# First layer's queries normalised chunk by chunk inside the projection, and turned ahead of the gating products

## The reference, cut to what matters

```
proj = h @ w_in[layer]                       # 2048 x 5632
u, v_sgu, za, q, k, v, zb = split(proj)      # 1024,1024,1024,1024,256,256,1024 columns
q = rope(rms_norm(heads(q, 8), q_norm_w))    # context rows: no rope
k = rope(rms_norm(heads(k, 2), k_norm_w))
attn = softmax(q k^T / sqrt(128)) v
s = w_sgu @ rms_norm(gelu(v_sgu), v_norm_w) + b_sgu
y = concat([gelu(u) * s * silu(za), attn * silu(zb)]) @ w_out[layer]
```

## Time and profile before

| | us |
|---|---|
| median of 3 runs (4398.26 to 4411.34) | 4401.06 |
| profiled execution, its time | 4397.11 |
| profiled execution, its span | 4395.3 |
| PE busy | 4023.3 (92%) |
| PE weight loads busy | 3134.3 (71%) |
| DVE busy | 2200.5 (50%) |
| ACT busy | 1661.2 (38%) |
| POOL busy | 139.8 (3%) |

### The profile page before, as it was taken

The page is one execution under the profiler, slowest core; times in us unless marked ns, Lnnn a source line. Parts: engine busy times, 40 slices in busy tenths (PEclk is TensorE's granted clock), DMA queues, the critical chain, the costliest instruction groups (busy, mean ns, idle before and its releaser), DMA issues. The chain is left out here.

```text
span 4395.3 us, 50269 instructions
## 1 busy us (share of the span) xinstructions
PE 4023.3 (92%) x20175; PEld 3134.3 (71%) x20175; DVE 2200.5 (50%) x3220; ACT 1661.2 (38%) x2270; POOL 139.8 (3%) x246
## 2 busy tenths in 40 slices
PE   5699999789799799977889999999995899999998
PEld 2466657668688688634677788888885777888887
DVE  6611123463544764375555555455547455554554
ACT  4221112341343444322224454354443445544543
POOL 2000000000000000002110000000000000000000
PEclk8799999899999999997769999999997999999999
DMA  9566555203265166532325565665561555656664
GB/s 355 184 214 206 196 183 172 92 24 120 72 192 166 64 213 196 158 115 90 117 84 169 145 186 191 187 185 188 189 219 59 183 175 144 186 190 189 186 198 162
DMA packets 351933, 719.05 MB, mean 164 GB/s; under 512 B 24478, under 2 KB 26874, under 8 KB 346858
## 3 DMA queue, kind: packets, MB, share of 16 engines
q1 hardware_dynamic: 331872, 637.74, 46.3%
q0 software_dynamic: 18192, 76.35, 5.1%
q10 hardware_dynamic: 1672, 2.24, 0.1%
HBM read 686.33 MB, written 26.48 MB: 162 GB/s over the span
## 5 line engine op out<-in xcount | busy, mean ns | idle before, releaser
L2187 DVE TENSOR_TENSOR ring_r<-ring,ring_r 128x1024 fp32r<-128x1024 f32 (+1 forms) x984 | 1189.6, 1218 | 1677.7 <-ACT ring_r L1496 1653.9
L1496 ACT ACTIVATE ring_r<-ring 128x1024 fp32r<-128x1024 f32 (+1 forms) x984 | 1029.6, 1053 | 1796.3 <-DMA ring<-in_w_in 587.2
L862 PE MATMUL acc<-ring_r,feat_hi 128*128 128x512 f32 x5120 | 1598.9, 394 | 32.3 <-DVE modc L2569 14.7
L862 PEld LDWEIGHTS acc<-ring_r,feat_hi 128*128 128x128 f32 x5120 | 956.5, 189 | 282.9 <-issue 32.1
L862 PE MATMUL acc<-ring_r,feat_lo 128*128 128x512 f32 x2560 | 1000.3, 391 | 0.0
L862 PE MATMUL acc<-ring_r,hid_t_hi 128*128 128x512 f32 x2048 | 631.5, 390 | 0.0
L862 PEld LDWEIGHTS acc<-ring_r,feat_lo 128*128 128x128 f32 x2560 | 482.7, 189 | 102.6
L862 PEld LDWEIGHTS acc<-ring_r,hid_t_hi 128*128 128x128 f32 x2048 | 383.7, 188 | 79.3
L862 PE MATMUL acc<-ring_r,hid_t_lo 128*128 128x512 f32 x1024 | 398.5, 389 | 0.0
L862 PE MATMUL acc<-ring_r,feat_e_hi 128*128 128x512 f32 (+1 forms) x1088 | 332.2, 388 | 17.1 <-DVEq L2275 9.8
L862 PEld LDWEIGHTS acc<-ring_r,feat_e_hi 128*128 128x128 f32 x1088 | 204.7, 191 | 58.3 <-issue 12.0
(11 more groups left out here) (453 smaller groups left out, 3268.4 us busy)
## 6 DMA issues: line engine op xcount, KB each, us to landing
ring<-in_ffn_up SPq DMA_DIRECT2D x256, 512.0 KB, 3.7
ring<-in_ffn_down SPq DMA_DIRECT2D x256, 512.0 KB, 3.9
ring<-in_w_mod SPq DMA_DIRECT2D x192, 512.0 KB, 5.4
ring<-in_w_in SPq DMA_DIRECT2D x176, 512.0 KB, 3.8
ring<-in_w_out SPq DMA_DIRECT2D x64, 512.0 KB, 3.7
ring<-in_even_w_in SPq DMA_DIRECT2D x64, 512.0 KB, 3.6
ring<-in_xattn_wkv SPq DMA_DIRECT2D x32, 512.0 KB, 5.4
ring<-in_even_w_out SPq DMA_DIRECT2D x32, 512.0 KB, 3.6
```

Source lines behind the costliest of these rows:

```text
L862: mm = pe.matmul(bank[0:l.shape[-1], 0:width], l, r, start=(kk == 0 and j == 0), stop=(kk == g.kt - 1 and j == len(terms) - 1))
L1496: f(ring_r[:, slot, 0, 0:kt, 0:width], ring[:, slot, 1, 0:kt, 0:width], ACT.Copy) \
L2187: tt(lo, raw, hi, ALU.subtract).then_inc(sem("w_lo"), E.up("w_lo"))
```

## The change

- **ACT, chunks 6 and 7 of layer 0**: a chunk's four tiles go into four buffers (two of `prob`, two of `stage`). After the fourth, ACT forms the chunk's 16 square sums into a scratch `q_tmp` (in the place of `kvb`, free until the key chunk) and their roots, and reports four tiles through `za_ready`. The first copy of chunk 6 waits for the means of v (`ms_ready`), the first of chunk 7 for the four query writes.
- **DVE**: the means of v move from the hook of chunk 5 to the front of slot 1 of chunk 6 (layer 0 only). At slots 1 to 4 of the next chunk (7 for chunk 6's heads, the key chunk for chunk 7's) it normalises and, for tiles 0 and 1, rotates one tile's four heads, then lets POOL write them.
- **POOL**: the eight writes now send normalised rows. `stage_free` comes after the last of them; w_sgu also waits for the writes. `q_d` is read back as soon as PE has used slot 3 (counted from 0) of the last `zb` chunk, when the first half of the features is free.
- **After the projection, both layers**: PE turns w_sgu, then all keys, then all queries, and then multiplies the gate; DVE copies in that order and does the gate's steps after the copies. `qk_ready` comes once, at the end of `norm_early`.

```diff
@@ POOL
-                                dma(q_d[...], prob[:, t % 2], f"q_out{t % 2}")
+                                dma(q_d[...], (prob, stage)[t // 2][:, t % 2], f"q_out{t % 2}")
...
+                if l == 0:
+                    for j in range(2):
+                        pool.wait_ge(sem(f"q_out{j}"), 16 * 4)
                 dma(sgu_raw, I["w_sgu"][l].rearrange("g p q -> p g q"), "sgu_in")
...
-                    pool.wait_ge(sem("proj_done"), L.due("proj_done"))
-                    for j in range(2):
-                        pool.wait_ge(sem(f"q_out{j}"), 16 * 4)
+                    pool.wait_ge(sem("ring_free"), slots_done(gemms["b1_0"][-2], 1, KT // 2 // KS))
                     dma(qbs[0], q_d.rearrange("(t p) d -> p t d", p=P), "q_in")
@@ PE, after the projection
+                pe.wait_ge(sem("qk_ready"), E.due("qk_ready"))
+                for t in range(4):
+                    turn([kvb[:, t, j * HD:(j + 1) * HD] for j in range(2)])
+                if l == 0:
+                    pe.wait_ge(sem("q_in"), 16)
+                for t in range(tiles):
+                    for h in (0, 4):
+                        turn([qb[:, t, (h + j) * HD:(h + j + 1) * HD] for j in range(4)])
                 pe.wait_ge(sem("sgu_t_ready"), E.due("sgu_t_ready"))
...
-                for t in range(4):
-                    pe.wait_ge(sem("qk_ready"), E.due("qk_ready"))
-                    if t < tiles:
-                        for h in (0, 4):
-                            turn([qb[:, t, (h + j) * HD:(h + j + 1) * HD] for j in range(4)])
-                    turn([kvb[:, t, j * HD:(j + 1) * HD] for j in range(2)])
@@ ACT, chunks 6 and 7 of layer 0
-                        if n_q[0] >= 2:
-                            act.wait_ge(sem(f"q_out{n_q[0] % 2}"), E.due(f"q_out{n_q[0] % 2}", 16))
-                        f(prob[:, n_q[0] % 2], bank, ACT.Copy).then_inc(sem("act_free"), E.up("act_free"))
+                        q = (prob, stage)[t // 2][:, t % 2]
+                        if n_q[0] == 0:
+                            act.wait_ge(sem("za_used"), E.due("za_used", 2))
+                            act.wait_ge(sem("ms_ready"), E.seen["ms_ready"] + 1)
+                        if n_q[0] == 4:
+                            for j in range(2):
+                                act.wait_ge(sem(f"q_out{j}"), E.due(f"q_out{j}", 32))
+                        f(q, bank, ACT.Copy).then_inc(sem("act_free"), E.up("act_free"))
+                        n_q[0] += 1
+                        if t < 3:
+                            return
...
+                        for u in range(4):
+                            act.wait_ge(sem("act_step"), E.cnt["act_step"])
+                            for h in range(4):
+                                hs, at = slice(h * HD, (h + 1) * HD), 32 + 8 * u + heads.start + h
+                                f(q_tmp[:, 0, hs], (prob, stage)[u // 2][:, u % 2, hs], ACT.Square, accum_out=stat[:, at:at + 1]) \
+                                    .then_inc(sem("act_step"), E.up())
+                        act.wait_ge(E.last_sem(), E.last_count())
+                        f(by_tile(stat2), by_tile(stat), ACT.Sqrt, bias=eps[:, 0:1], scale=1.0 / HD).then_inc(sem("act_step"), E.up())
+                        act.wait_ge(E.last_sem(), E.last_count())
+                        for u in range(4):
+                            act.nop().then_inc(sem("za_ready"), E.count("za_ready"))
@@ ACT, after the projection
-                if l == 0:
-                    act.wait_ge(sem("q_in"), E.due("q_in", 16))
-                    (32 squares of qb and their roots)
@@ DVE, hooks
+                def behind(c):
+                    def q_heads(_, s):
+                        if c == 6 and s == 1:
+                            means_v(q_tmp[:, :, :].rearrange("p a b -> p (a b)"))
+                        t = s - 1
+                        if c >= 7 and 0 <= t < 4:
+                            dve.wait_ge(sem("za_ready"), E.due("za_ready"))
+                            first = 32 + 8 * t + 4 * (c - 7)
+                            r = stat2[:, first:first + 4]
+                            dve.reciprocal(r, r).then_inc(sem("dve_step"), E.up())
                             dve.wait_ge(E.last_sem(), E.last_count())
+                            norm_heads(t, 0, blocks((prob, stage)[t // 2][:, t % 2], HD), r, q_tmp[:, 1])
+                            dve.wait_ge(E.last_sem(), E.last_count())
+                            dve.nop().then_inc(sem("q_chunk"), E.count("q_chunk"))
+                            dve.nop().then_inc(sem("za_used"), E.up("za_used"))
+                        if c == 8 and t == 3:
+                            dve.nop().then_inc(sem("stage_free"), E.count("stage_free"))
+                    return q_heads if l == 0 and c >= 6 else None
@@ DVE, after the projection: the 4 key copies and 2 query copies a tile stand
   ahead of the gate's steps; reciprocal and norm_heads of the queries are gone there
```

More of the change, by code:

```diff
@@ L283, in two_blocks @@
         kvb = view(28672, 4, 512)
+        q_tmp = view(28672, 2, 512)
         q_ts = [view(8192, 8, 4 * P), view(8192, 8, TT * P)]
@@ L377, in two_blocks, with slots_done @@
                 n_split += g.n * g.slots if g.split else 0
+        def slots_done(last, chunk, slots):
+            done = 0
+            for st in ORDER:
+                for g in gemms[st]:
+                    if g is last:
+                        return done + chunk * (g.slots - 1) + slots
+                    done += g.n * (g.slots - 1) * (1 + len(g.riders))
         def b1_units(layer):
@@ L1708, in project, with keep_kv @@
                 elif kind == "kv":
-                    act.wait_ge(sem("za_used"), E.due("za_used", 2))
-                    evac(n, lambda c, cs, t, bank: f(kvb[:, t], bank, ACT.Copy).then_inc(sem("act_free"), E.up("act_free")))
+                    def keep_kv(c, cs, t, bank):
+                        if t == 0:
+                            act.wait_ge(sem("za_used"), E.due("za_used", 2 if len(item) > 3 else 8))
+                        f(kvb[:, t], bank, ACT.Copy).then_inc(sem("act_free"), E.up("act_free"))
+                    evac(n, keep_kv)
                 else:
@@ L2187, in take_lo, with stream @@
                 tt(lo, raw, hi, ALU.subtract).then_inc(sem("w_lo"), E.up("w_lo"))
-            def stream(g, hook=None, counts=(), unroll=False):
+            def stream(g, hook=None, counts=(), unroll=False, each=None):
                 nonlocal g_n, t_n
@@ L2195, in chunk @@
                     for s in range(g.slots):
+                        if each:
+                            each(c, s)
                         if s == max(g.slots - 2, 0) and hook:
@@ L2544, in _, with project @@
             dve.nop().then_inc(sem("trig_args"), E.count("trig_args"))
-            def project(item, hook=None):
+            def project(item, hook=None, each=None):
                 nonlocal t_n
@@ L2578, in project @@
                 else:
-                    stream(n, hook, unroll=True)
+                    stream(n, hook, unroll=True, each=each)
             def s5_first():
@@ L2609, in gate_u @@
                         tt(m, m, stage[:, ((c - 4) * tiles + t) % 2], ALU.mult).then_inc(sem("za_used"), E.up("za_used"))
[L2610 removed]
+                    if c == 5 and l:
                         dve.wait_ge(E.last_sem(), E.last_count())
[L2612 to L2618 removed]
+                        means_v(stage[:, :, :].rearrange("p a b -> p (a b)"))
+                        dve.nop().then_inc(sem("stage_free"), E.count("stage_free"))
@@ L2637, in block1, with norm_heads @@
                 sq = prob[:, :, :].rearrange("p a b -> p (a b)")
-                def norm_heads(t, w):
-                    v, n, r = ((blocks(kvb[:, t, 0:256], HD), 2, stat2[:, 64 + t * 2:66 + t * 2]) if w else
-                               (blocks(qb[:, t], HD), 8, stat2[:, 32 + t * 8:40 + t * 8]))
+                def norm_heads(t, w, v, r, rot):
+                    n = v.shape[1]
                     tt(v, v, along(r, HD), ALU.mult).then_inc(sem("dve_step"), E.up())
@@ L2694, in block1 @@
                 dve.nop().then_inc(sem("sgu_t_ready"), E.count("sgu_t_ready"))
+                for t in range(4):
+                    dve.tensor_copy(k_t[:, :, t * P:(t + 1) * P],
+                                          turned()[:, 0:2 * P].rearrange("p (k t) -> p k t", t=P)) \
+                                              .then_inc(sem("tp_free"), E.up("tp_free"))
+                for t in range(tiles):
+                    for h in range(2):
+                        dve.tensor_copy(q_t[:, h * 4:h * 4 + 4, t * P:(t + 1) * P],
+                                              turned()[:, :].rearrange("p (k t) -> p k t", t=P)) \
+                                                  .then_inc(sem("tp_free"), E.up("tp_free"))
+                dve.wait_ge(E.last_sem(), E.last_count())
+                dve.nop().then_inc(sem("qkt_ready"), E.count("qkt_ready"))
```

60 lines of the change are left out of this document (18 added, 42 removed).

## The result

The changed kernel takes 4368.81 us (median of 6 runs, 4361.69 to 4375.99), the kernel before 4403.07 in the same comparison: a ratio of 0.9923, interval 0.991 to 0.9937, 34 us less. One of the six runs of the kernel before took 14795.77 us; the median of the other five is 4401.06, and against that the change takes 32 us. On a second chip the changed kernel (five runs, 4364.26 to 4374.07) and the kernel before gave 4366.33 and 4403.44 (0.992, 0.9907 to 0.9934), 37 us less. The forecast was 4363, 38.3 us less, with a range of 4351 to 4375. The profiled execution took 4371.63 us with a span of 4369.8.

The account below looks back on a forecast made before the run. PE, busy 92% of the span, was taken as the bound, so only stretches where it stands could give much. 30.1 + 5.0 + 7.5 - 2.3 - 2.0 = 38.3 us off 4401.06 gave 4362.8, about 4363; range 4351 to 4375.

Parts of the forecast that it names:

- chunk 6: stop: Start of chunk 6: with v's means moved out of chunk 5, PE resumes at 574.54 instead of 580.11, 5.57 us gained.
- chunk 6: clock behind it: Rest of the slot behind chunk 6's stop: 2.94 us at 2.4 GHz instead of 4.91, 1.97 us gained.
- chunk 7: longer stop: Start of chunk 7: ACT's squares, table load and root lengthen PE's stop from 2.5 to 4.8 us, 2.3 lost.
- chunk 7: clock: Behind chunk 7's stop of 4.8 us: the clock was assumed to fall, another 2.0 us lost (0 to 2).
- new work in chunks 6 to 8: Added DVE and ACT work, beyond the longer stop at chunk 7, fits beside the projection's slots at cost 0.
- layer 0's tail, to the exponential: After layer 0's projection: chain removed and reordered, first exponential at 860.1 instead of 890.19, 30.1 us gained (25 to 31).
- Cover: Spare time: 4 us ahead of the key chunk's slot 2; query read landing by 824 or 832, needed at 843.
- layer 1's tail, to the exponential: After layer 1's projection: the same reordering without a missing norm, 5.0 us gained (3 to 5.5).
- the tail overlaps badly: Rival: products, steps and copies alternate at the low clock, layer 1 gains 3; 31 us gained, 4370; chance 0.14.
- The step that failed: Start of layer 0's attention: PE's first score some 2 us ahead of DVE's maximum, hiding ACT's table load.

Follow-up runs that it names:

- e5: The changed kernel plus 24 transposes of the identity, which nobody reads, after PE's first two scores in layer 0's attention; 4368.44 us, ratio 0.9925.
- e1: The changed kernel with the means of v's squares back in the hook of chunk 5; 4376.42 us, ratio 0.9942.
- e4: The changed kernel with ACT's squares and roots of chunks 6 and 7 moved behind the last two slots' high halves; 4366.89 us, ratio 0.9923.
- the same kernel: The changed kernel itself, unaltered, profiled on the second chip; its median there is 4366.33 us.
- e8: The changed kernel with chunk 7's 16 squares made three times over; one run, 4379.6 us, against 4408.11 for the kernel before.
- e2: The changed kernel with the read of the queries issued after the projection, as before the change; 4371.2 us, ratio 0.9931.
- e6: The changed kernel with the last two w_out low halves made inside attention and proj_done set after ACT's last evacuation, both layers; 4356.65 us, ratio 0.9901.
- e7: The changed kernel with the edits of e4, e5 and e6 together; 4353.08 us, ratio 0.9889.
- e3: The changed kernel with keys and queries turned behind the gating products again and copied behind the gating steps, both layers; 4375.19 us, ratio 0.9938.

## Why the prediction was right, and where it was off

The mechanisms were the ones forecast, and the sum nearly so, in two places by some luck, named below. Term by term, from the profiles:

| step | forecast | measured | how |
|---|---|---|---|
| chunk 6: stop | 5.57 | 5.33 | 7.78 - 2.45 |
| chunk 6: clock behind it | 1.97 | 1.96 | 4.91 - (575.61 - 572.66) |
| chunk 7: longer stop | -2.3 | -2.4 | 2.51 - 4.91 |
| chunk 7: clock | -2.0 | -1.6 | 2.94 - (644.53 - 639.99) |
| new work in chunks 6 to 8 | 0 | 0 | under Cover |
| layer 0's tail, to the exponential | 30.1 | 29.6 | 46.15 + 1.34 - 16.98 - 0.91 |
| clock in layer 0's attention | not foreseen | -2.9 | 5.49 - 8.40, e5 |
| layer 1's tail, to the exponential | 5.0 | 4.0 | 15.35 - 11.34 |
| sum | 38.3 | 34.0 | |

**Chunk 6** held to 0.3 us, and e1 shows the cause by putting it back.

**Chunk 7**: the stop forecast at 4.8 us measured 4.91, and e4 shows that the squares and the table load lengthen it. The clock fell, as assumed, but not for the reason that I gave, a delay shorter than the stop: the window from 640 to 641 has 0.63, which puts the fall at about 640.3, 5.2 us after PE's last product and after it had resumed at 639.99. In all eight executions with a stop of 4.9 us there the clock fell, in three of them (after, the same kernel, e8) after PE had resumed. That term came out by some luck. The load took 1.28 us, and the root began at 635.70, 0.02 after its end. No drain stands between them, so the rule of the Trainium skill (ScalarE: Activation LUTs, "What ACT_TABLE_LOAD costs"), by my estimate 1.4 us more, does not hold here.

**Cover.** From PE's resuming in chunk 7 to the first copy of the gating weights it took 281.03 - 85.31 = 195.7 us before and 277.83 - 80.43 = 197.4 after; the difference is the 1.6 of the clock. So squares, root, norm, writes and the read cost nothing between. e8 puts the cover ahead of the key chunk at 4.0 us, e2 shows the read's use. That read took 10.0 us from issue to landing and was issued at 809.8:

```profile
L602 POOL DMA_DIRECT2D big<-q_d x1: 750/750/750, 809.8 to 809.8; - x1
...
DMA to landing us min/median/max: 2.3/2.6/10.0
```

It landed by 820, some 19 us ahead of PE's first turn of a query row. Issued that early, under the last chunk's loads, it took 9.1 to 11.1 us in nine executions; behind the projection it took 8.7 in the kernel before and 8.1 in e2. With the statement of the Trainium skill (DMA: Bandwidth & Descriptors, "Issuing engines are not separate DMA queues") that DMAs of different issuing engines run on the same 16 DMA engines, the traces agree in direction. A delay of the loads does not show in the first copy (e2).

**Layer 0's tail.** The 0.5 missing are the 12 copies: 838.67 to 845.71 is 7.04 us, where I had put 6.45. PE began its 36 blocks at the lower clock and set their pace at the start; in e6, at full clock throughout, the copies took 0.6 less. That is the rival "the tail overlaps badly" at a tenth of its price. My 0.171 us a block "even at the low clock" was misread: in that row the clock was back at about 884.7 (the window from 884 to 885 has 0.64), and the blocks ahead of it started 0.21 us apart, those behind 0.11. That PE's turning took 6.04 us, near my 6.2, is luck: the clock came back at about 841.7 (the window from 841 to 842 has 0.67). At the lower clock 36 blocks would have taken 7.7, an estimate from the 0.21.

**The step that failed** is what I put behind the first maximum: "PE's first score then lies some 2 us ahead of DVE's maximum and not behind it". That was so, and I counted its good side (the table load hidden, 0.43 us in each layer) but not the other: a PE that is ahead stands, and at the start of attention, where DVE then waits for PE's products (its third maximum stood 1.54 us for a score), the clock fell. It is 2.9 us, the largest part of the 4.3 missing, and a term that my sum had at nothing. I had listed three falls of the clock and applied them to chunk 7 alone.

**Layer 1's tail** is 1.0 short: copies and maximum came 0.8 later than my sum for the same reason as in layer 0 (the copies from 1442.80 to 1447.4 took 4.6, not 3.81), the rest is gaps.

**What I did not ask.** I took the w_out low half ahead of the tail as fixed ("what precedes it is the low half of the last w_out slot ... and neither moves"). It did not move, but it could have: e6 moves it and gets 9.7 us, more than layer 1's reordering gives. What stays open: by the marks e6 and e7 reach layer 1's first maximum 14 and 18 us ahead of the changed kernel on that chip, while their medians gain 9.7 and 13.3. The changed kernel's profiled execution was its slowest of five there (4374.07 us), e6's its fastest of four (4353.99), which is part of it; what makes one execution of a kernel some us longer than the next was not found.

## What to carry to other kernels

When work is moved off a chain, ask of each engine that is now ahead what it does while it stands: PE's idle time may be free and the clock behind it not; here 2.8 us of free idle time cost up to 2.9 us of work. Look at where the clock comes back inside a row, too, before a rate is taken from it. And read what stands directly in front of the chain's first instruction on its engine: the queue order there had put a prefetch ahead of the critical copies, and taking it away won more than a quarter of what the whole change had. Gains of 3 to 4 us in a kernel whose runs spread over 10 are seen by marks in a profile counted from a place ahead of the edit, and hardly by medians.

## What the hardware did that I had not expected

The clock's fall is not decided by the length of PE's stop alone. The first pair of matmuls after a stop tells it (0.73 us at 2.4 GHz, 1.22 at 1.2, between them where it changed in the pair). At the start of chunk 6 it took 0.73 after stops of 2.45, 2.13, 2.53, 1.73, 2.20 and 2.07 us (after, the same kernel again, e2, e4, e5, e8), but 1.22, 1.03 and 1.08 after 2.33, 2.20 and 1.86 (e3, e6, e7). At chunk 7 it took 0.73 after 2.51 before and 2.14 in e7, and 1.09 after 2.05 in e4. So at a stop of about 2 us either happens, and no edit here controlled which; a fall costs up to 2 us more. Nor is the delay from PE's last product to the fall one number: in the kernel after it was 5.2 us at chunk 7 and 2.0 at attention.
